# Latent attention with the largest scores taken one unit ahead, a query product in passes, and a gated recurrence whose norms are full sums

## What is computed

```python
def mla_attention(c_q, c_kv, k_r, q_norm_g, kv_norm_g, w_uq, w_ukv, cos, sin):
    q = (rms_norm(c_q, q_norm_g) @ w_uq).reshape(B, S, MLA_HEADS, MLA_NOPE + MLA_ROPE)
    ...
    def block(args):                       # 8 heads, 128 queries at a time
        s = (q_nope . k_nope + q_rope . k_rope) * scale
        p = jax.nn.softmax(s, axis=-1)
        return jnp.einsum('bhqk,bkhd->bqhd', p.astype(v.dtype), v)

def _hgrn2_mixer(q, f_fwd_raw, f_bwd_raw, i, g, lb, norm_g):
    ...
    o = _gla_chunk_forward(q4, k_f, i4, lf_f) + flip(_gla_chunk_forward(flip(q4), ...))
    o = _rmsnorm(o, norm_g) * jax.nn.silu(heads(g))      # norm over the 128 values of a head

def _rwkv7_mixer(p, ..., g2, ...):
    g = jax.nn.sigmoid(gd) @ g2                          # 128 x 512, four tiles of rows
    ...
    y = (y + bonus) * g
```

## Time and profile before

| | us |
|---|---|
| median of 3 runs | 2756.87 (2755.76 to 2760.75) |
| the profiled execution | 2744.78 |
| its span, first to last instruction | 2742.8 |
| mean granted clock of PE | 0.965 of 2.4 GHz |

### The profile page before, as it was taken

How to read it: one execution, slowest core, us unless ns; L and a number is a source line. 1 busy time by engine, 2 the same in 40 slices (tenths; PEclk the granted TensorE clock), 3 DMA queues, 4 the chain that set the end, 5 groups by cost and what they waited for, 6 DMA issues and landing times. The chain is left out here.

```text
span 2742.8 us, 44702 instructions
## 1 busy us (share of the span) xinstructions
PE 2559.9 (93%) x19048; PEld 2062.0 (75%) x19072; DVE 1507.2 (55%) x2230; ACT 945.3 (34%) x1419; POOL 283.0 (10%) x232
## 2 busy tenths in 40 slices
PE   8999999999999988999879896999989998999898
PEld 7888765678887666788658785788878776788786
DVE  3474387543753776446356565755455496545532
ACT  4223225433232245443444342343322323433321
POOL 0000030010000300200333130100003000000011
PEclk9999999999999999999989999899999998999999
DMA  4232223113232231223200001432325111232231
GB/s 140 93 100 92 94 95 133 62 63 100 95 98 101 93 135 49 71 92 100 82 1 4 3 4 40 177 99 93 126 105 215 62 64 62 78 106 93 87 115 52
DMA packets 56394, 238.20 MB, mean 87 GB/s; under 512 B 6592, under 2 KB 7360, under 8 KB 47616
## 3 DMA queue, kind: packets, MB, share of 16 engines
q1 hardware_dynamic: 56192, 235.30, 24.6%
HBM read 231.08 MB, written 4.19 MB: 86 GB/s over the span
## 5 line engine op out<-in xcount | busy, mean ns | idle before, releaser
L348 PE MATMUL banks<-b_h,pin_pair 128*128 128x512 f32 x2304 | 528.3, 390 | 0.0
L348 PEld LDWEIGHTS banks<-b_h,pin_pair 128*128 128x128 f32 x2304 | 431.1, 188 | 89.0
L348 PE MATMUL banks<-ffh,ff_pair 128*128 128x512 f32 x2016 | 457.3, 389 | 0.0
L348 PEld LDWEIGHTS banks<-ffh,ff_pair 128*128 128x128 f32 x2016 | 378.3, 188 | 78.7
L348 PE MATMUL banks<-b_h,pab_pair 128*128 128x512 f32 x792 | 180.7, 390 | 2.3 <-DVE pab_pair L334 2.3
L348 PEld LDWEIGHTS banks<-b_h,pab_pair 128*128 128x128 f32 x792 | 148.4, 188 | 33.4 <-DVE pab_pair L334 2.7
L2868 DVE TENSOR_TENSOR ff<-ff_c,ff 128x512 fp32r<-128x512 f32 x44 | 30.5, 692 | 204.8 <-ACT ff L2856 203.4
L334 DVE TENSOR_TENSOR pin_pair<-pin_raw,pin_pair 128x1024 fp32r<-128x1024 f32 x50 | 61.3, 1226 | 135.0 <-ACT pin_pair L327 135.0
L334 DVE TENSOR_TENSOR pin_pair<-first,pin_pair 128x1024 fp32r<-128x1024 f32 x50 | 61.3, 1226 | 126.9 <-ACT pin_pair L327 126.9
L327 ACT ACTIVATE ff_pair<-ff_raw 128x1024 fp32r<-128x1024 f32 x58 | 61.5, 1059 | 182.5 <-PE banks L348 182.5
L1220 DVE SCALAR_TENSOR_TENSOR x<-banks,modf,x 128x512 f32<-128x512 f32 x32 | 24.0, 750 | 172.7 <-PE banks L366 172.7
(11 more groups left out here) (543 smaller groups left out, 4588.2 us busy)
## 6 DMA issues: line engine op xcount, KB each, us to landing
ff_raw<-in_ffn_up SPq DMA_DIRECT2D x58, 512.0 KB, 3.7
pin_raw<-in_w_in SPq DMA_DIRECT2D x50, 512.0 KB, 3.5
first<-in_w_in SPq DMA_DIRECT2D x48, 512.0 KB, 3.5
dn_raw<-in_ffn_down SPq DMA_DIRECT2D x16, 1408.0 KB, 7.4
dil_ada_ring<-in_ada_w SPq DMA_DIRECT2D x20, 1024.0 KB, 7.0
first<-in_ffn_up SPq DMA_DIRECT2D x30, 512.0 KB, 3.8
mla_ada_ring<-in_ada_w SPq DMA_DIRECT2D x12, 1024.0 KB, 9.7
pab_raw<-in_ab_in SPq DMA_DIRECT2D x23, 512.0 KB, 3.5
```

The source lines that it names most:

```text
L348: mm = nc.tensor.matmul(bank, w(a, k), x(b, k), start=k == 0 and i == 0, stop=k == kt - 1 and i == 2)
```

## The change

In latent attention DVE takes the largest scores and the shift of unit u+1 ahead of the reciprocal and the scaling of unit u, for u from 1 on; for u = 0 the next unit's follow its scaling. PE's unit loop stays as it is. The products of the first contraction tile of the query product run in three passes over the six output tiles, each behind a wait for what it reads.

In the gated recurrence the sums for the norm are one product with a full 128 x 128 matrix of ones, so each partition holds each token's sum; ACT takes logarithm and exponential (x to the power -1/2) of it in place of root, reciprocal, spreading and transposition. The end decays of the second set are made at the start. The gate rows, with the load of g2, move into the first `rwkv_units`, where g2 lies in the buffer y1 for the time.

```diff
@@ mla_attention, PE @@
-                for k in range(nq):
+                pe.wait_ge(high, 1)
+                pe.wait_ge(lifted, 1)
+                for a, b in ((0, 0), (0, 1), (1, 0)):
+                    if b:
+                        pe.wait_ge(left, 1)
+                    if a:
+                        pe.wait_ge(fine, 1)
+                    for t in range(q_tiles):
+                        query(0, t, a, b)
+                for k in range(1, nq):
                     pe.wait_ge(fine, k + 1)
                     pe.wait_ge(left, k + 1)
@@ mla_attention, DVE @@
-                for u in range(units):
-                    pair, i, s = u // TT, u % TT, 2 * (u % 2)
+                def largest(u):
+                    i, s = u % TT, 2 * (u % 2)
                     dve.wait_ge(scored, u + 1)
+                    if u >= 2:
+                        dve.wait_ge(weighed, 2 * u - 2)
                     chain.step(nc.vector.tensor_reduce(top[:, u % 2], m.ps[:, s:s + 2], AX_X, ALU.max))
                     nc.vector.tensor_scalar(shift[:, u % 2], top[:, u % 2], q_minus[:, i:i + 1], None, ALU.mult)\
                         .then_inc(reduced, 1)
+
+                largest(0)
+                for u in range(units):
+                    pair, i, s = u // TT, u % TT, 2 * (u % 2)
+                    if 1 <= u < units - 1:
+                        largest(u + 1)
...
                             .then_inc(evened, 1)
+                    if u == 0:
+                        largest(1)
@@ hgrn, ACT @@
+                def logarithm(h):
+                    act.wait_ge(totalled, h + 1)
+                    nc.scalar.activation(root_h(h), m.ps[:, 6 + h % 2], ACT.Ln, bias=m.eps[:, 0:1], scale=1.0 / P)\
+                        .then_inc(logged, 1)
+
                 def root(h):
-                    act.wait_ge(totalled, max(2, h + 1))
...
+                    act.wait_ge(logged, h + 1)
+                    nc.scalar.activation(root_h(h), root_h(h), ACT.Exp, scale=-0.5).then_inc(rooted, 1)
 
                 powers(0)
                 ends(0)
+                powers(1)
+                ends(1)
...
@@ hgrn, ACT, behind the loop over sets (s == 5 ends with logarithm(0), s == 6 with root(0)) @@
+                square(2)
+                logarithm(1)
+                logarithm(2)
+                square(3)
+                logarithm(3)
                 root(1)
-                square(2)
                 root(2)
-                square(3)
                 root(3)
@@ hgrn, DVE @@
                 lower_ends(0)
+                lower_ends(1)
                 for i in range(PAIRS):
+                    if i == 2:
+                        decay(0)
@@ hgrn, PE @@
+                    nc.tensor.matmul(m.ps[:, 6 + h % 2], m.ones[:], sq[:, h % 2], start=True, stop=True)\
+                        .then_inc(totalled, 1)
...
-                    if s % 2 == 1:
-                        gate_sums(s // 2)
...
+                totals(2)
                 values(sets - 1)
-                pe.wait_ge(placed_r, PAIRS)
-                stretch(0)
-                stretch(1)
-                totals(2)
                 totals(3)
-                stretch(2)
-                stretch(3)
@@ rwkv_units, first direction: SP, PE, ACT @@
+                    sp.dma_start(g2, m.tables["rwkv_g2"]).then_inc(g2_in, 16)
...
+                    pe.wait_ge(g2_in, 16)
+                    for i in range(PAIRS):
+                        nc.tensor.matmul(m.ps[:, 4 + i], g2[:, i * P:i * P + P], rr[:, 14], start=True, stop=True)\
+                            .then_inc(gated, 1)
...
-                    dc.powers(act, 0, 1)
+                    for i in range(PAIRS):
+                        if i == 2:
+                            dc.powers(act, 0, 1)
+                        act.wait_ge(gated, i + 1)
+                        nc.scalar.activation(m.mix[:, 4 + i], m.ps[:, 4 + i], ACT.Copy).then_inc(placed, 1)
```

More of the change, by code:

```diff
@@ L965, in mix, with query @@
                     mm.then_inc(used, 1)
-                for k in range(nq):
+                def query(k, t, a, b):
+                    col = HEADS * NOPE + t * P if t < 2 else (t - 2) * P
+                    return nc.tensor.matmul(m.ps[:, t], uq[:, a, k, col:col + P], low[:, b, k],
+                                            start=k == 0 and (a, b) == (0, 0),
+                                            stop=k == nq - 1 and (a, b) == (1, 0), skip_group_check=True)
+                pe.wait_ge(high, 1)
[8 more added lines that the diff above has]
+                for k in range(1, nq):
                     pe.wait_ge(fine, k + 1)
@@ L970, in _ @@
                     for t in range(q_tiles):
-                        col = HEADS * NOPE + t * P if t < 2 else (t - 2) * P
                         for a, b in ((0, 0), (0, 1), (1, 0)):
-                            mm = nc.tensor.matmul(m.ps[:, t], uq[:, a, k, col:col + P], low[:, b, k],
-                                                  start=k == 0 and (a, b) == (0, 0),
-                                                  stop=k == nq - 1 and (a, b) == (1, 0), skip_group_check=True)
+                            mm = query(k, t, a, b)
                         if k == nq - 1:
@@ L1843, in _ @@
                 for s in range(sets):
-                    if s + 1 < sets:
+                    if 1 <= s and s + 1 < sets:
                         ends(s + 1)
@@ L1857, in _ @@
                                 .then_inc(logged_k, 1)
+                        act.wait_ge(kept, 16)
+                        logarithm(0)
                     if s == 6:
@@ L1951, in _ @@
                     nc.vector.tensor_tensor(w.kkt[:, i], w.kkt[:, i], norm_k(i), ALU.mult).then_inc(normed_k, 1)
-                widen(0)
-                widen(1)
+                scale(0)
                 gate(3)
-                scale(0)
-                scale(1)
-                widen(2)
-                scale(2)
-                widen(3)
-                scale(3)
+                for h in range(1, AH):
+                    scale(h)
             @block.tensor
@@ L1980, in scores @@
                     if s == 0:
-                        pe.wait_ge(blocks_in, 16)
-                        for i in range(PAIRS):
-                            pe.wait_ge(squared_k, i + 1)
-                            pe.wait_ge(placed_v, i + 1)
-                            nc.tensor.matmul(m.ps[:, 4 + i], w.blocks, norm_k(i), start=True, stop=True)\
-                                .then_inc(summed_k, 1)
+                        key_sums()
                     pe.wait_ge(levelled, 6 * s + 6)
@@ L2224, in rwkv_units @@
         weighted, dotted, bonused = sem("weighted"), sem("dotted"), sem("bonused")
+        g2_in, gated, placed = sem("g2_in"), sem("gated"), sem("placed")
         dc.open(sem)
```

90 lines of the change are left out of this document (29 added, 61 removed).

## The result

The changed kernel takes 2859.6 us (median of 4 runs, 2857.1 to 2864.6) against 2756.7 us before (4 runs, 2755.8 to 2760.8): ratio 1.037, 95% interval 1.035 to 1.039, or **102.9 us slower**. I had forecast 81 us, and a range that ended at 2856; the time lies 3.5 us above its upper end. The direction and the mechanism were right; two terms of the sum were not, the half clock and the gain of the recurrence.

The account below looks back on a forecast made before the run. The prediction took PE, busy 93% of the span, to bound the kernel. It summed +62.0 (ring) + 32.4 (clock) - 1.4 (query) - 12.1 (recurrence) = +80.9 us, for a median of 2838 us, range 2800 to 2856.

Parts of the forecast that it names:

- Ring: Latent attention's unit loop: score, largest scores, scaling and flip wait on each other in turn; 31.0 us more per layer.
- The clock: Latent attention's loop: PE's waits in units with a fold bring the half clock; 32.4 us more in all.
- flip 1.02 and score 1.06 + 1.17, 3.25 us: Latent attention, units with a fold: the PE work on which the half clock would lie, doubling its 3.25 us.
- The upper bound, 39 us: Latent attention's half clock: most it could cost, 3.25 us in each of twelve units with a fold.
- Rival E: Latent attention: half clock through the whole loop, 51 us a layer on top of the 31, median 2907; chance 5%.
- Query: Query product in three passes: PE starts up to 1.35 us earlier, 0.7 us gained a layer, 1.4 in all.
- Recurrence: Gated recurrence, loop and tail: 12.1 us gained, bounds 6 and 17.
- POOL would otherwise run through: Gated recurrence, second set: with end decays at the front POOL runs on, so PE's 4.70 us wait goes.
- the 2.5 us for the half clock: Gated recurrence: the half clock behind PE's 4.70 us wait goes with it, 2.5 us gained.
- the 1.8 us for the gate rows: Gated recurrence: gate-row products leave PE; two groups count with 0.9 us each, 1.8 us gained.
- RWKV, 0: First RWKV units: the added g2 load and four products and copies cost 0 us, bounds -1 and +4.
- Rival C: Latent attention: score(u+1) lies done when DVE comes to it, so DVE's 1.7 us waits go; median 2729, chance 7%.

Follow-up runs that it names:

- e4: e1 with identity products on PE, unused by the result, where it would stand still: 2821.1 us against 2747.1 for the kernel before, ratio 1.027.
- e6: The changed kernel with PE issuing score(u+2) in pass u instead of score(u+1): 2725.7 us against 2755.6 for the kernel before, ratio 0.989.
- h1: The kernel before with only the recurrence's second-set end decays, and the decay table with them, moved to the front: 2742.0 us against 2747.1, ratio 0.998.
- h2: h1 with the gate rows also moved to the first RWKV units: 2751.1 us against 2758.6 for the kernel before, ratio 0.997.
- e5: e1 with the fold moved behind the scaling of its unit: 2783.6 us, ratio 1.013 to the kernel before.
- e1: The kernel before with only DVE's new order in latent attention (largest scores moved ahead): 2859.7 us against 2755.6, ratio 1.037.
- e7: The kernel before with only PE's order changed, issuing score(u+2) in pass u: 2743.5 us against 2747.1, ratio 0.999.
- e8: e6 with only the end decays' move to the front kept of the recurrence's edits: 2731.7 us against 2758.6 for the kernel before, ratio 0.991.
- e9: e6 measured again on another chip, with all edits of the change: 2727.6 us against 2758.6 for the kernel before, ratio 0.989 to 0.990.
- e2: The kernel before with only the query product's first tile in three passes: 2750.3 us against 2755.6, ratio 0.998.
- e3: The kernel before with only the edits of the gated recurrence and first RWKV units: 2753.5 us, ratio 0.999.

## Why the prediction was partly right

- **Ring: right, step by step.** 31.0 us a layer foretold, 30.4 measured without the clock (e4). 8.26 and 5.36 us for the two kinds of unit foretold, 8.29 and 5.39 measured. In the kernel after, L929 to L1119 is 1.17, scaling to flip 0.54, fold 2.90, each as in the earlier trace rows.
- **Where PE would stand still: right.** 4.1 to 4.4 us foretold in units with a fold, 4.05 (502.13) and 4.32 (a unit earlier, at 484.22) measured.
- **The clock: right that it falls, mis-sized.** I took 2.7 us for each of six units with a fold, 16.2 a layer. The loop has 117.95 - 92.8 = 25.2 us of it, if all that goes beyond the ring is put down to the clock: 6.5 in the six units with a fold (56.8 us together, by the sum of the prediction 50.4) and 18.7 in the seven without. The step that failed is that the half clock would lie on "flip 1.02 and score 1.06 + 1.17, 3.25 us". It didn't end there: mix and the next flip, which in a unit without a fold have no waiting beside them, ran at 0.50 as well (the whole 8.16 us of the window 467.81, against 5.36). The upper bound, 39 us for both layers, was too low by the same step, and so was the range. Rival E, half clock throughout the loop, had 51 us a layer, twice what was measured; by the mean of 0.70 the half clock holds for 60% of it.
- **Clock, the rule.** The Trainium skill ("TensorE: Matmul & The Clock Gate", section "HAM oscillation — how this bites in real kernels") says that short bursts with waits between them start cold each time. With all 39 us by that rule I would have given 2845; the trace agrees with it (the flips behind the 4 us waits) and goes further, with 49 to 50 us. Its rule on transpositions ("Part 4: PE-mode transpose"), which stood behind rival E, is not tested here: e6 has its loop at 1.00 with a fourth of PE's time in flips, but the other three fourths are other products, and the products added in e4 are plain ones.
- **Query: right in the timeline, and too small to see in the time.** PE's first product starts 0.9 us behind the start of ACT's L1030 (L1018 before) instead of 2.2. The timeline's rows:

```profile
417.41 0.85 ACT L1030 ACTIVATE mla_uq<-first 128x768 fp32r<-128x768 f32 x1 [10.89 <-PEq L68]
...
418.31 2.07 PE L969 MATMUL banks<-mla_low,mla_uq 128*128 128x512 f32 x4 [2.14 <-ACT mla_uq L1030]
...
418.63 0.95 DVE L1082 TENSOR_TENSOR mla_uq<-first,mla_uq 128x768 fp32r<-128x768 f32 x1
```

  It no longer waits for DVE's L1082, which comes later. The first score product comes 0.8 us sooner from the stage's start (437.90 - 417.1 against 431.11 - 409.5); I had said 0.7.
- **Recurrence: half.** 12.1 foretold, 5.9 measured, just under the lower bound of 6. Against the stage's start (1337.9 before, 1461.4 after) PE's product behind the end decays comes 4.3 us earlier in set 1, 5.2 in set 2, and no more than 4.7 in set 7. Its rows:

```profile
1478.14 0.68 PE L1990 MATMUL banks<-hg_qh,hg_kh 128*64 128x64 f32 x8
...
1480.35 2.66 POOL L1796 TENSOR_TENSOR hg_kh<-hg_ke,hg_weights 128x256 f32<-128x256 f32 x3 [3.06 <-DVE hg_ke L1906]
...
1482.97 2.65 POOL L1796 TENSOR_TENSOR hg_qh<-hg_qd,hg_weights 128x256 f32<-128x256 f32 x3
...
1485.68 0.68 PE L1990 MATMUL banks<-hg_qh,hg_kh 128*64 128x64 f32 x8 [2.51 <-POOL hg_qh L1796]
...
1511.37 0.75 DVE L1906 SCALAR_TENSOR_TENSOR hg_ke<-hg_ke,lb,hn 128x512 f32<-128x512 f32 x1 [5.50 <-ACT hg_ke L1817]
...
1515.79 1.12 PE L1990 MATMUL banks<-hg_qh,hg_kh 128*64 128x64 f32 x8 [3.04 <-POOL hg_qh L1796]
...
1519.56 1.92 PE L2017 MATMUL banks<-hg_at,hv 128*128 128x128 f32 x8
...
1527.02 0.75 DVE L1923 SCALAR_TENSOR_TENSOR b_mix<-banks,params,hgt 128x512 f32<-128x512 f32 x1 [6.37 <-PE banks L2023]
...
1530.32 1.28 ACT L1838 ACT_TABLE_LOAD   x1
...
1532.28 1.89 DVE L1929 TENSOR_TENSOR b_mix<-b_mix,x 128x512 f32<-128x512 f32 x3 [4.51 <-ACT x L1838]
```

  The 4.70 us stall went as foretold (1478.14 has no wait). The step that failed is "**POOL would otherwise run through**": with PE and DVE earlier, POOL itself waits 3.06 us for DVE's key and then needs 2.66 and 2.65 us for what took 1.76 a set earlier, so PE waits 2.51 us for POOL one set on. So the 2.5 us for the half clock and the 1.8 us for the gate rows came off the work of an engine that waits for POOL anyway; h1 and h2, which differ by the gate rows, have stages of 73.6 and 73.9. The last set sets the limit: there PE waited 2.31 us for POOL already in the kernel before (at 1397.02). I had that wait only as unchanged, not as one that takes back what PE saves ahead of it. In the kernel after, POOL waits there for DVE's L1906, which waits 5.50 us for ACT's end decays. What PE saves in the sets between only makes its own wait longer, 3.04 us now. In the tail the gating came 3.5 us earlier (1527.02; I had said 9.5), since the last set comes only 4.7 us earlier and PE, after the 3.04 us wait at 1515.79, runs it at half clock (L2017 1.92 us instead of 1.05). From the last square to the end it takes 6.4 us; I had worked out 6.2.
- **RWKV, 0: right** within 1 us in the kernel after. Over all profiles the stage takes 131.6 to 134.6 us with the gate rows in it (five kernels, 133.3 on the mean) and 131.4 to 133.2 without them (eight, 132.4), which doesn't allow a finer statement.
- **The sum.** 62.0 foretold and 61 shown for the ring; 32.4 and about 49 for the clock; -12.1 and -5.9 for the recurrence. These make up the 22 us by which the forecast was short, to within 1 us: 17 are the clock's, 6 the recurrence's. Rival C (faster) had its deciding point right: whether score(u+1) ends before the exponentials of unit u do. e6 puts it on that side, with -30 us where I had worked out -27 for it.

## What to carry to other kernels

When an instruction is moved ahead on one engine, write down the order of the engine that feeds it: if the feeder's queue has, ahead of the operand, something that needs what now stands behind the moved instruction, the two alternate and nothing overlaps. The remedy was one more unit of lead on the feeder. DVE's edit alone cost 104 us, PE's alone gave 4; both with the rest of the change gave 30. And where such a ring makes TensorE stand still for 4 us, price the half clock for all that TensorE does in the unit behind the wait (here the whole 8.16 us at 467.81), not for the few matmuls right behind it: in this loop it ended only while TensorE was at work again, and a wait never ended it.

## What the runs showed that I had not expected

- A short wait can be followed by the half clock in one place and not in another. In the kernel before PE waits 1.43 us ahead of unit 2 (444.97) and runs on at 1.00; in the kernel after it waits 1.44 ahead of the same product (451.77) and runs on at 0.71 on the mean. The rows, columns as above:

```profile
444.97:449.13 4.16, 4.16 (x32) 2.31 (x32) 1.89 (x5) 1.32 (x3) 0.00 (x0) 1.00 0.00 0
```

```profile
451.77:456.00 4.23, 4.23 (x24) 2.17 (x24) 1.68 (x4) 1.15 (x3) 0.00 (x0) 0.71 0.00 0
```

  PE's work just before differs by little, and no run here isolates the reason. In the 13 steps of e5 the clock holds behind every wait of 1.15 and 1.16 us and falls at every one of 2.43 and 2.44.
- Identity products, of no use to the result, are a gain by themselves: e4 has 576 matmul instructions more than e1 and loses 74 us against the kernel before, where e1 loses 104.
- The stage of dilated attention, the same in all kernels, takes 99.5 to 100.1 us or 105 to 107 (table above), with more of it at half clock in the longer ones. Two windows over it, the kernels before and after:

```profile
310.00:409.50 99.50, 92.60 (x1012) 66.70 (x1024) 76.72 (x111) 20.16 (x22) 29.14 (x12) 0.96 0.31 118
```

```profile
310.00:417.10 107.10, 99.09 (x1024) 70.05 (x1024) 72.71 (x111) 19.97 (x22) 36.65 (x12) 0.92 0.29 110
```

  Same work, PEclk 0.96 and 0.92, and POOL busy 29.1 and 36.7 us for 12 instructions. It goes with the chip rather than with the kernel. On the chip of e4, e5, e7 and h1 all eight such stages are short, on that of h2, e8 and e9 all six are long, and on that of e1, e2, e3 and e6 the first is long in all four and the second in e1 alone. The kernel before has a median of 2747.1 us on the first, 2758.6 on the second and 2755.6 on the third. So a time is to be set against one from the same chip, and a profile may come from another than the runs. Whether that is why the profile before lay 12.1 us under its median isn't shown: both its stages are short, but e5's profiled execution has both short as well and lies 9.8 us above its kernel's median. Why the chips differ stays open.
- POOL and DVE take longer beside each other. POOL's three products of L1796 take 1.76 us or, beside DVE's steps of the next set, 2.66; DVE's L1906 takes 0.74 us at 1479.47, when POOL stands idle, and 1.10 at 1483.48 beside POOL. No run here isolates it, but DVE work brought forward can come to lie beside POOL's and lengthen both.
